# Memory attention of an encoder kernel: scores placed into the query projection, part of the output projection into the last head, layers written out

## Reference

```
def memory_attention(h, mem_h, w_mq, w_mkv, w_mo):
    q = (h @ w_mq).reshape(B, S, MEM_HEADS, MEM_HEAD_DIM)
    kv = (mem_h @ w_mkv).reshape(B, -1, 2, MEM_HEADS, MEM_HEAD_DIM)
    k, v = kv[:, :, 0], kv[:, :, 1]
    s = jnp.einsum('bqhd,bmhd->bhqm', q, k) * (MEM_HEAD_DIM ** -0.5)
    p = jax.nn.softmax(s, axis=-1)
    o = jnp.einsum('bhqm,bmhd->bqhd', p, v).reshape(B, S, D_MODEL)
    return o @ w_mo
```

## Time and profile before

| | |
|---|---|
| median of 3 runs | 1600.33 us |
| profiled execution | 1602.88 us, of which the span of its instructions is 1601.1 us |
| mean granted TensorE clock | 0.970 |
| TensorE busy | 1488.0 us, 93% |
| VectorE, ScalarE, GpSimd busy | 773.9, 760.9, 696.0 us |

### The profile page before, as it was taken

How to read it: one execution, slowest core, us unless ns; L and a number is a source line. 1 busy time by engine, 2 the same in 40 slices (tenths; PEclk the granted TensorE clock), 3 DMA queues, 4 the chain that set the end, 5 groups by cost and what they waited for, 6 DMA issues and landing times.

```text
span 1601.1 us, 20864 instructions
## 1 busy us (share of the span) xinstructions
PE 1488.0 (93%) x6846; PEld 1215.6 (76%) x6846; DVE 773.9 (48%) x1264; ACT 760.9 (48%) x1187; POOL 696.0 (43%) x327
## 2 busy tenths in 40 slices
PE   4988879998999999999999787999989999999995
PEld 3766658877878888888877565798778888888883
DVE  4547767815165431255162866783423654114543
ACT  5676645536254432344356765463634443224431
POOL 3374415840434454434536362376123534544350
PEclk9998899999999999999999888999999999999997
DMA  4320013530213332222322101244111323322221
GB/s 167 116 66 27 14 53 119 184 105 1 97 61 106 105 111 100 80 89 94 123 92 94 41 14 40 82 155 148 50 53 66 103 94 105 117 94 85 86 79 53
DMA packets 39048, 138.91 MB, mean 87 GB/s; under 512 B 4848, under 2 KB 5104, under 8 KB 38704
## 3 DMA queue, kind: packets, MB, share of 16 engines
q1 hardware_dynamic: 37440, 134.23, 24.7%
q10 hardware_dynamic: 1520, 3.52, 0.7%
HBM read 135.64 MB, written 2.10 MB: 86 GB/s over the span
## 4 chain that ended last, share of the span: by engine, by line
PE 50%; issue 30%; POOL 17%; DVE 1%; ACT 1%; POOLq 0%; DVEq 0%; ACTq 0%
PE ps L1316 16%; PE ps L1317 16%; PE ps L1318 16%; POOL w_lo L342 12%; POOL arena L362 1%; POOL work L355 1%; POOL work L356 1%; POOL work L357 1%; POOL h_lo L367 0%; PE ps L1466 0%; DVE work L1299 0%; DVE work L885 0%; ACT arena L556 0%; ACT work L533 0%; PE ps L1326 0%
## 5 line engine op out<-in xcount | busy, mean ns | idle before, releaser
L342 POOL TENSOR_TENSOR w_lo<-raw,w_hi 128x1024 fp32r<-128x1024 f32 x248 | 603.1, 2449 | 768.5 <-ACT w_hi L444 767.0
L1316 PE MATMUL ps<-h_hi,w_hi 128*128 128x512 f32 (+2 forms) x1040 | 409.4, 394 | 25.4 <-POOL w_lo L342 22.4
L444 ACT ACTIVATE w_hi<-raw 128x1024 fp32r<-128x1024 f32 x248 | 255.6, 1055 | 323.5 <-PE ps L1318 322.4
L1318 PE MATMUL ps<-h_hi,w_lo 128*128 128x512 f32 (+2 forms) x1040 | 405.1, 390 | 0.0
L1317 PE MATMUL ps<-h_lo,w_hi 128*128 128x512 f32 (+2 forms) x1040 | 405.0, 389 | 0.0
L1316 PEld LDWEIGHTS ps<-h_hi,w_hi 128*128 128x128 f32 (+1 forms) x1040 | 196.1, 189 | 69.4 <-issue 22.6
L1316 PE MATMUL ps<-arena,w_hi 128*128 128x512 f32 (+2 forms) x656 | 247.7, 378 | 0.0
L1317 PE MATMUL ps<-arena,w_hi 128*128 128x512 f32 (+2 forms) x656 | 245.3, 374 | 0.0
L1318 PE MATMUL ps<-arena,w_lo 128*128 128x512 f32 (+2 forms) x656 | 244.5, 373 | 0.0
L1317 PEld LDWEIGHTS ps<-h_lo,w_hi 128*128 128x128 f32 (+1 forms) x1040 | 196.1, 189 | 41.0 <-issue 1.0
L1318 PEld LDWEIGHTS ps<-h_hi,w_lo 128*128 128x128 f32 (+1 forms) x1040 | 196.0, 188 | 40.8
(11 more groups left out here) (175 smaller groups left out, 1913.4 us busy)
## 6 DMA issues: line engine op xcount, KB each, us to landing
raw<-blocks_d SPq DMA_DIRECT2D x248, 512.0 KB, 3.3
x<-xT_d SPq DMA_DIRECT2D x4, 512.0 KB, 8.7
work<-memT_d ACTq DMA_DIRECT2D x2, 1024.0 KB, 4.9
outT_d<-work SPq DMA_DIRECT2D x8, 256.0 KB, 2.2
work<-ln_d ACTq DMA_DIRECT2D x2, 512.0 KB, 3.4
par<-par_d ACTq DMA_DIRECT2D x2, 113.5 KB, 2.0
work<-pos_d ACTq DMA_DIRECT2D x1, 128.0 KB, 7.0
mix_g<-par_d ACTq DMA_DIRECT2D x2, 4.0 KB, 6.6
```

The lines of the kernel that those rows point to most:

```text
L342: gp.tensor_tensor(w_lo[:, b % SPLIT, :], raw[:, b % RAW, :], w_hi[:, b % SPLIT, :].bitcast(F32), ALU.subtract).then_inc(lo_done.sem, 1)
L444: act.activation(w_hi[:, b % SPLIT, :], raw[:, r, :], ACT.Copy).then_inc(hi_done.sem, 1)
L1316: pe.matmul(out, a_hi, b_hi, start=first, stop=False)
L1318: return pe.matmul(out, a_lo, b_hi, start=False, stop=last)
```

## The change

Four things, all in the memory attention but the last:

- TensorE makes the scores of steps 0 to 3 ahead of the last block of the query projection (B_MQ+7). They need query subtractions 1 to 4; scores of later heads need 2h+2. ScalarE's copies and VectorE's subtractions of the second four query tiles move behind exponentials 0 to 2 and scaling 0, and behind maxima 0 to 3.
- The first half of the output projection is cut into 8 parts of one k-step (output_part, 12 matmuls). Parts 0 to 3 stand in steps 12 to 15, each behind its turn (in step 13 behind attend 2 too), the other four after the last attend.
- Banks: scores 0 to 3, turned probabilities 4 and 5, attends 6 and 7. ScalarE's splits of B_MO+3 and B_MO+4 stand at the end of steps 11 and 15 in place of behind the loop.
- The loop over the two layers is written out on TensorE, ScalarE, VectorE and GpSimd.

```diff
-        BM, BO = (0, 1, 6, 7), (4, 6, 7, 5)
+        BM, BO = (0, 1, 2, 3), (4, 6, 7, 5)
...
-            with gp.Fori(0, DEPTH) as l:
+            for l in range(DEPTH):
                 layer(l)
...
-                for g in range(2):
-                    for b in range(B_MQ + 4 * g, B_MQ + 4 * g + 4):
-                        ahead(b)
-                    queries(g)
-
+                for b in range(B_MQ, B_MQ + 4):
+                    ahead(b)
+                queries(0)
+                for b in range(B_MQ + 4, B_MQ + 8):
+                    ahead(b)
...
                 act.preload_act_table_set("natural_log_exp_and_others")
                 for i in range(3):
                     mexps(i)
                 mprobs(0)
+                queries(1)
                 for i in range(MEM_HEADS * TT):
...
                     mturned_hi(i)
                     if t == 2 and h >= 1:
                         outputs(h - 1)
+                    if (h, t) == (2, 3):
+                        ahead(B_MO)
+                    if (h, t) == (3, 3):
+                        ahead(B_MO + 1)
                 outputs(MEM_HEADS - 1)
-                for b in range(B_MO, B_MO + 5):
+                for b in range(B_MO + 2, B_MO + 5):
                     ahead(b)
...
+                queries_lo(0)
...
                 for i in range(4):
                     mmax(i)
                 recip(0)
                 recip(1)
+                queries_lo(1)
...
-                project(B_MQ + 4, BB, h_hi, h_lo, lambda k: None, tile_mm=mq_mm)
-

                 def mscores(i):
                     h, t = divmod(i, TT)
+                    if i < 4:
+                        need(qml_done, max(2, i + 1))
+                    elif t == 0:
+                        need(qml_done, 2 * h + 2)
                     if i >= 4:
                         need(mexp_done, i - 3)
...
                 def mturn(i):
                     need(mprob_done, i + 1)
-                    if i >= 2:
-                        need(pml_done, i - 1)
+                    need(*((pml_done, i - 1) if i >= 2 else (qml_done, 5 + i)))
...
                 def mattend(h):
                     need(pml_done, TT * h + TT)
-                    if h >= 1:
-                        need(oml_done, 2 * h)
+                    need(*((oml_done, 2 * h) if h >= 1 else (qml_done, 8)))
...
-                need(qml_done, 8)
-                for i in range(4):
-                    mscores(i)
+                def first_mscores():
+                    for i in range(4):
+                        mscores(i)
+
+                project(B_MQ + 4, BB, h_hi, h_lo, lambda k: None, between=first_mscores, tile_mm=mq_mm)
+
+                def output_part(k):
+
+                    b = B_MO + k // 2
+                    if k % 2 == 0:
+                        block_ready(b)
+                    need(oml_done, k + 1)
+                    wh, wl = halves(b, 512)
+                    for j in range(4):
+                        if k == 0:
+                            need(mexp_done, 13 + j)
+                        c = slice(P * j, P * j + P)
+                        last = product3(ps[BA[j]][:, :], wh[:, k % 2, c], wl[:, k % 2, c], qm_hi[:, k, :],
+                                        qm_lo[:, k, :], k == 0, k == KD - 1)
+                    if k % 2 == 1:
+                        last.then_inc(used.sem, 1)
...
                     mturn(i)
                     if t == 1 and h >= 1:
                         mattend(h - 1)
+                    if h == MEM_HEADS - 1:
+                        output_part(t)
                 mattend(MEM_HEADS - 1)
-                project(B_MO, BA, qm_hi, qm_lo, lambda k: need(oml_done, k + 1))
+                for k in range(4, KD):
+                    output_part(k)
                 project(B_MO + 4, BB, qm_hi, qm_lo, lambda k: None)
```

More of the change, by code:

```diff
@@ L726, in mturned_hi @@
                     act.activation(pm_hi[h % 2][:, :, P * t:P * t + P],
-                                   ps[2 + i % 2][:, 0:MT * P].rearrange("p (k q) -> p k q", k=MT), ACT.Copy)\
+                                   ps[4 + i % 2][:, 0:MT * P].rearrange("p (k q) -> p k q", k=MT), ACT.Copy)\
                         .then_inc(pmh_done.sem, 1)
@@ L732, in outputs @@
                         need(mpv_mm, 2 * h + j + 1)
-                        act.activation(qm_hi[:, 2 * h + j, :], ps[4 + j][:, :], ACT.Copy)\
+                        act.activation(qm_hi[:, 2 * h + j, :], ps[6 + j][:, :], ACT.Copy)\
                             .then_inc(omh_done.sem, 1)
@@ L805, in layer @@
                                 hi_and_square(l, MIX, t, 24 + t + 1, later=1)
-            with act.Fori(0, DEPTH) as l:
+            for l in range(DEPTH):
                 layer(l)
@@ L1176, in layer, with queries_lo @@
                 values_lo(1)
-                for g in range(2):
+                def queries_lo(g):
                     for j in range(4):
@@ L1190, in mturned_lo @@
                     c = slice(P * t, P * t + P)
-                    dve.tensor_tensor(pm_lo[h % 2][:, :, c], ps[2 + i % 2][:, 0:MT * P].rearrange("p (k q) -> p k q", k=MT),
+                    dve.tensor_tensor(pm_lo[h % 2][:, :, c], ps[4 + i % 2][:, 0:MT * P].rearrange("p (k q) -> p k q", k=MT),
                                       pm_hi[h % 2][:, :, c].bitcast(F32), ALU.subtract).then_inc(pml_done.sem, 1)
@@ L1196, in outputs @@
                         need(omh_done, 2 * h + j + 1)
-                        dve.tensor_tensor(qm_lo[:, 2 * h + j, :], ps[4 + j][:, :],
+                        dve.tensor_tensor(qm_lo[:, 2 * h + j, :], ps[6 + j][:, :],
                                           qm_hi[:, 2 * h + j, :].bitcast(F32), ALU.subtract).then_inc(oml_done.sem, 1)
@@ L1288, in layer @@
                 assert count[0] == N_STEP, count[0]
-            with dve.Fori(0, DEPTH) as l:
+            for l in range(DEPTH):
                 layer(l)
@@ L1598, in mturn @@
                     need(mprob_done, i + 1)
-                    if i >= 2:
-                        need(pml_done, i - 1)
+                    need(*((pml_done, i - 1) if i >= 2 else (qml_done, 5 + i)))
                     for k in range(MT):
-                        last = pe.transpose(ps[2 + i % 2][:, P * k:P * k + P], em[:, i % 4, P * k:P * k + P], ident[:, :])
+                        last = pe.transpose(ps[4 + i % 2][:, P * k:P * k + P], em[:, i % 4, P * k:P * k + P], ident[:, :])
                     last.then_inc(mturned.sem, 1)
@@ L1613, in mattend @@
                             at = 2 * k + f // 4
-                            last = product3(ps[4 + j][:, :], vm_hi[:, at, c], vm_lo[:, at, c],
+                            last = product3(ps[6 + j][:, :], vm_hi[:, at, c], vm_lo[:, at, c],
                                             pm_hi[h % 2][:, k, :], pm_lo[h % 2][:, k, :], k == 0, k == MT - 1)
                         last.then_inc(mpv_mm.sem, 1)
-                need(qml_done, 8)
-                for i in range(4):
-                    mscores(i)
+                def first_mscores():
[16 more added lines that the diff above has]
+                        last.then_inc(used.sem, 1)
                 for i in range(MEM_HEADS * TT):
@@ L1670, in layer @@
                                 blocks=GROUPS[half])
-            with pe.Fori(0, DEPTH) as l:
+            for l in range(DEPTH):
                 layer(l)
```

## The result

| | before | after |
|---|---|---|
| median | 1599.42 us (4 runs, 1597.85 to 1602.95) | 1582.32 us (4 runs, 1581.26 to 1583.34) |
| profiled execution | 1602.9 us, span 1601.1 (one of before's longer ones, see e5) | 1582.8 us, span 1580.3 |
| mean granted clock | 0.970 | 0.972 |

The ratio is 0.9884 with a 95% interval of 0.9866 to 0.9902, or 16 to 21 us faster. The forecast of 1584.0 is 1.7 us too high.

A forecast was written before the change was run, and what follows sets the result against it. TensorE bounds it (busy 1488 of 1601.1 us), so gains are its waits and slow clock. Per layer 2.4 - 0.5 + 3.0 + 3.3 = 8.2, by whole lengths 8.0; 8.0 taken twice gives a 1584 us median, range 1577 to 1592.

The forecast's parts named there:

- First scores in the query block: Start of the memory attention stretch: early scores remove PE's waits of 1.6 and 0.8, gain 2.4 us per layer.
- Middle: Waits of 0.3 to 0.5 before turns 2, 3, 4, 5, 8, 9: together 2.4 against 1.9, loss 0.5 per layer.
- Output parts: Steps 12 to 15 and last attend: waits of 4.7 shrink to 1.7 (1.2 and 0.5), gain 3.0 us per layer.
- Clock: Both slow-clock stretches near the end of the memory attention go, clock 1.00 throughout, gain 3.3 us per layer.
- a fall after turn 12 in after: Rival: clock still falls once per layer after the 1.2 and 0.5 waits, 2.3 more per layer, 1588.6; chance 0.22.
- Whole stretch: From B_MQ+7 to the output projection's second half: 65.4 us falls to 57.4, 8.0 less per layer.
- DMAs, POOL, banks: Splits of B_MO+3 and B_MO+4 about 15 us earlier cost 0; other banks cost nothing beyond the stepped waits.
- Layers in full: Written-out layer loops: PE's jump of up to 3.39 us is covered by its queue, register arithmetic mostly hidden; gain 0.
- Rival, instructions arrive late: PE's straight code of the second layer waits for instruction packets, slower, 1635 if all uncovered; chance 0.03.
- Sum: 8.2 per layer by terms, 8.0 by whole lengths; 8.0 taken twice, 16.0 us, for a median of 1584.
- mixers of another length: Sign of being wrong: all other stages should keep their length; changed mixers would be the work of layers in full.

The follow-up runs named there:

- e5: Before's kernel with the layer loop written out on ScalarE alone: 1597.39 us, ratio 0.9988.
- e4: After's kernel without early scores (scores 0 to 3 behind the query block, query copies and subtractions in old places), output parts kept: 1583.13 us, ratio 0.9893.
- e3: After's kernel with the first half of the output projection whole again behind the last attend, its two splits behind the loop: 1589.16 us, ratio 0.9928.
- e13: Before's kernel with after's banks for scores, turned probabilities and attends, order and loops as before: 1598.91 us, ratio 0.9996.
- e2: Before's kernel with the layer loops written out on all four engines and nothing else: 1598.0 us, ratio 0.9982.
- e6: Before's kernel with the layer loop written out on TensorE, VectorE and GpSimd, not on ScalarE: 1598.17 us, ratio 0.9992.
- e9: After's kernel with head 1's output copies and subtractions moved to step 12, B_MO+3's split to step 13, part 1 ahead of attend 2: 1576.02 us, ratio 0.9853.
- e12: e9's kernel unchanged, measured again in the group of e10: 1576.88 us, ratio 0.9855.
- e11: e9's kernel with e10's table load put in: 1579.72 us, ratio 0.9874.
- e0: After's kernel unchanged, measured again in the group of e9: 1581.60 us, ratio 0.9889.
- e1: After's kernel with the four loops over the layers kept as loops: 1584.18 us, ratio 0.9897.
- e10: After's kernel with one ScalarE table load put back at the head of layer 1: 1582.67 us, ratio 0.9890.

## Why the prediction was right, and where it was off

- **First scores in the query block**: right. Forecast gain 2.4 less 0.5, e4 measures 2.05.
- **Middle**: right. Short waits of 0.2 to 0.4 before turns 2, 3, 4, 5, 8 and 9 add up to 1.9 in after, and to 1.4 in before when they are counted in the same way (starts less 0.118 after a score). The forecast had 2.4 and 1.9, the latter with the pipeline's restarts in it, so the loss of 0.5 was right. Both this and the place of turn 0 came from stepping the queues with durations of before.
- **Output parts**: right. The wait before turn 12 (1.1 against 1.2), the wait in part 0 (0.37 against 0.5), none at the last attend. From e3 to after 4.8 per layer, against 4.65 by the terms.
- **Clock**: right in its size for before, since e4 gains 6.3 against 3.0 + 3.3. The rival, a fall after turn 12 in after, did not come: 1.00 in both layers' windows. But the trace of before alone had made the two waits of 1.1 look like the cause of its first fall; e3 has the same two and no fall behind them. That they are enough by themselves is refuted, and what else it takes is open. So the rule by which I called the clock, from the lengths of the waits, is not shown, and that the forecast of 1.00 came true was in part luck.
- **Whole stretch**: 57.0 against 57.4, 8.4 per layer against 8.0.
- **DMAs, POOL, banks**: 0, right. The earlier splits delay nothing: the second half of the output projection keeps its 38.1 without a wait, the MLP its 361.1. e13 gives 0.9996 for the banks.
- **Layers in full**: the one term of the sum that was mis-sized. I took 0, weighing PE's jump and the register arithmetic, and did not look at the loop heads of the other engines. Measured: 1.2 to 1.6 at the first matmul, from ScalarE's table load of 1.28. Before's trace had the row at 16.74; nothing was asked of it. About PE's jump the argument held: with it gone attention and MLP keep their length within 0.1 (e2, e6). Whether PE's written-out loop keeps the longer executions away is open (see e5). The Trainium skill (Runtime: NRT & Kernel Launch, Instruction fetch mechanics) has a taken branch to a target outside the fetched pages stall the engine until that is fetched; the jump does take 3.39 us, but e6's interval ends at 2.7 and the MLP in which it lies is no shorter, so here the queue of issued matmuls hides it.
- **Rival, instructions arrive late**: did not come. The layers in full take 48 packets of instructions where the loops took 52, and layer 2's attention takes the 219.79 of layer 1:

```profile
q8 instruction: 48, 0.79, 0.2%
```

- **Sum**: 16.7 from the attention and some 1.5 from the start make 18.2, against 17.1 by the medians and 18.5 by the ratio. The difference is within what the mixers and the start vary. They were forecast at no change, and on this scale they aren't fixed. So a median 1.7 from the forecast is in part luck; the 8.4 per layer in the stretch is what bears the account out. For the same reason mixers of another length were no sign of the written-out layers' work, as I had put it: e9 and e12 differ in them and are one kernel.

## What to carry to other kernels

Where a pipelined loop runs out of its own cover, the next product's matmuls that are ready can be dealt out one part per step; their worth is the waits they fill plus the slow clock that those waits bring. The waits can be stepped beforehand from durations in the old trace; the clock can't be counted on in the same way, as e3 had the same two waits of 1.1 and no fall behind them. A loop written out may change more than its jump: look for a table load, or any other preparation, at the head of each engine's loop, and ask who waits behind it. Judge a change of a few microseconds by windows between marks of the stage it touches: e4 lacks 4.1 us of gain and its median shows 0.8 to 1.5 of that, e9 showed 5.6 for an edit worth 2.2. And look at the single times before the median: before's fall into two groups.

## What the runs showed that I had not expected

- **Identical mixers take 184.6 to 188.9 us.** The length goes with the time at 1.2 GHz inside them: with 27.3 us of it 184.6 to 185.8 (both layers of e3, e4 and e9, layer 2 of e2, e6, e11 and e12), with 30.7 to 34.1 us 186.4 to 188.9 (both layers of before, after, e0, e1, e5 and e10, layer 1 of the others); e13's layer 2, with 23.9, took 185.5. Layer 2's came out alike in after, e0 and e10 (187.05, 186.87, 186.96) and in e9, e11 and e12 (184.75, 184.79, 184.79), layer 1's did not. But the order of the attention does not fix them: with before's order they took 188.94 in before and e5 and 185.6, 185.8 and 185.5 in e2, e6 and e13, and with after's order and the loops kept (e1) 187.65. What sets them is open. A shift of the start by 1.3 us (e10) didn't, and nothing else was tried.
- **An earlier first matmul is not always an earlier first mark.** e9 and e12 are one kernel. Their first matmuls start at 19.98 and 19.88, their first marks at 39.36 and 37.87. PE waits for nothing between, but e9's matmuls start 0.43 apart until 26.06, e12's only until 23.00. First e9, then e12:

```profile
23.10 0.63 PE L1326 MATMUL ps<-h_lo,w_hi 128*128 128x512 f32 x1
23.53 0.63 PE L1327 MATMUL ps<-h_hi,w_lo 128*128 128x512 f32 x1
```

```profile
23.25 0.39 PE L1327 MATMUL ps<-h_hi,w_lo 128*128 128x512 f32 x1
23.48 0.39 PE L1325 MATMUL ps<-h_hi,w_hi 128*96 128x512 f32 x1
```

Over all fourteen traces this lasts from 3.1 to 6.1 us after the first matmul, worth up to 1.5 at the first mark, as much as the table load. So e5, without the load, has its first mark at 39.58 and e6, with it, at 39.93.

- **The same waits do not always bring the same clock.** 1.1 and 1.1 us were followed by a fall in before and by none in e3, with the same matmuls between and behind them. Earlier in the stretch before has two waits that e3 hasn't, 1.6 and 0.8. e4 has those and one of 1.1, and no fall. The five traces with all four waits (before, e2, e5, e6, e13) have two slow stretches, 6.8 us at 1.2 GHz, in each layer. That fits that all are needed; where in time they stood was not varied by itself, so it isn't shown.
- **A table load of 1.28 us at a loop's head.** It appears in both passes of ScalarE's loop and goes when that loop alone is written out (e5), not with the other three (e6). Presumably what the engine holds on entry differs between the passes, so it is loaded at each; that is an argument, not a measurement.
